# Memory projection between the steps of the causal latent attention; token sums of squares made on PE

## The reference, cut to what matters

```python
mla_out = _rms_norm(_latent_attention(q_m, k_m, v_m), mla_out_g[l])      # 8 heads, causal
x = x + jnp.concatenate([diff_out, mla_out], axis=-1) @ w_out[l]
x = x + _memory_cross_attention(_rms_norm(x, norm_cross_g[l]), _rms_norm(mem, norm_mem_g[l]),
                                w_mem_q[l], w_mem_kv[l], w_mem_o[l])
x = x + _hierarchical_moe(_rms_norm(x, norm_ffn_g[l]), ...)
...
x = _rms_norm(x, norm_final_g)          # end of the first block
h = rms_norm(x, ln_mix[0])              # start of the second
proj = h @ w_in                         # 3072 + 12 + 256 columns; the 12 are the gates b and a
```

## Time and profile before

| | |
|---|---|
| median of 3 runs | 2022.97 us (2021.37 to 2024.80) |
| the profiled execution's own time | 2024.49 us |
| its span in the profile | 2022.2 us |
| PE busy | 1881.0 us (93%) |
| DVE, ACT, POOL busy | 1056.4, 759.7, 123.1 us |
| instructions | 27340 |
| moved by DMA | 248.58 MB, 410 GB/s at most in a fortieth of the span |

### The profile page before, as it was taken

One profiled execution on the slowest core, in us unless ns is written; L12 is line 12 of the kernel. 1 busy time (PEld: TensorE's weight loads), 2 busy tenths in 40 slices (PEclk: granted clock), 3 DMA queues, 4 the chain that ended last, 5 costly groups with the idle time before them and its releaser, 6 DMA issues.

```text
span 2022.2 us, 27340 instructions
## 1 busy us (share of the span) xinstructions
PE 1881.0 (93%) x10882; PEld 1447.1 (72%) x10882; DVE 1056.4 (52%) x2003; ACT 759.7 (38%) x1606; POOL 123.1 (6%) x108
## 2 busy tenths in 40 slices
PE   6999888998997859999879999999999999999997
PEld 5665567786554437778777888888876688888886
DVE  6757656353211157775655444644567654444444
ACT  4455744441111146523443322322345542222222
POOL 0000000001212135010210000000000000000000
PEclk9999988999999969999999999999999999999998
DMA  5101213349999942122002233232321132323321
GB/s 192 43 10 31 89 45 110 141 149 400 410 410 408 402 173 74 61 66 74 2 1 85 90 103 94 86 112 89 99 73 43 32 105 94 104 92 95 95 94 42
DMA packets 72621, 248.58 MB, mean 123 GB/s; under 512 B 9218, under 2 KB 11522, under 8 KB 71600
## 3 DMA queue, kind: packets, MB, share of 16 engines
q1 hardware_dynamic: 67088, 235.65, 33.2%
q0 software_dynamic: 5408, 11.19, 1.6%
HBM read 242.62 MB, written 12.59 MB: 126 GB/s over the span
## 4 chain that ended last, share of the span: by engine, by line
PE 74%; DVE 7%; DMA 4%; ACT 3%; issue 1%; POOL 0%; DVEq 0%; POOLq 0%; SPq 0%; ACTq 0%
PE ps_pair L299 18%; PE ps_pair L300 18%; PE ps_pair L301 18%; PE ps_pair L2050 5%; DMA w_places<-w_experts 2%; PE ps_turn L2661 2%; PE ps_pair L892 1%; PE ps_out L2061 1%; PE ps_shared L2061 1%; DMA split_acts_as_f<-w_experts 1%; PE ps_out L923 1%; PE ps_pair L2653 1%; DVE g L2461 1%; PE ps_turn L904 1%; DMA g<-rows_h,g_as_int 1%
## 5 line engine op out<-in xcount | busy, mean ns | idle before, releaser
L299 PE MATMUL ps_pair<-split_acts,w_high 128*128 128x512 f32 (+1 forms) x1816 | 722.5, 398 | 25.0 <-DVE split_acts L626 13.2
L301 PE MATMUL ps_pair<-split_acts,w_low 128*128 128x512 f32 (+1 forms) x1816 | 706.0, 389 | 0.0
L300 PE MATMUL ps_pair<-split_acts,w_high 128*128 128x512 f32 (+1 forms) x1800 | 699.8, 389 | 0.0
L299 PEld LDWEIGHTS ps_pair<-split_acts,w_high 128*128 128x128 f32 x1816 | 344.5, 190 | 106.9 <-issue 27.2
L242 DVE TENSOR_TENSOR w_low<-w_raw,w_high 128x1024 fp32r<-128x1024 f32 (+4 forms) x249 | 281.6, 1131 | 258.2 <-ACT w_high L236 256.3
L301 PEld LDWEIGHTS ps_pair<-split_acts,w_low 128*128 128x128 f32 x1816 | 344.0, 189 | 72.2
L300 PEld LDWEIGHTS ps_pair<-split_acts,w_high 128*128 128x128 f32 x1800 | 342.3, 190 | 67.7 <-issue 1.9
L236 ACT ACTIVATE w_high<-w_raw 128x1024 fp32r<-128x1024 f32 (+4 forms) x249 | 242.8, 975 | 145.5 <-PE ps_pair L301 143.2
L372 DVE TENSOR_TENSOR x<-x,ps_pair 128x512 f32<-128x512 f32 x80 | 55.0, 687 | 140.6 <-PE ps_pair L301 140.6
L2288 DVE TENSOR_TENSOR g<-g,ps_pair 64x256 f32<-64x256 f32 x31 | 13.2, 425 | 177.1 <-ACT g L2232 177.1
L3254 ACT ACTIVATE split_acts<-h 128x512 fp32r<-128x512 f32 x44 | 27.9, 633 | 200.1 <-DVE h L3267 200.1
(11 more groups left out here) (562 smaller groups left out, 2392.9 us busy)
## 6 DMA issues: line engine op xcount, KB each, us to landing
w_raw<-w_gu SPq DMA_DIRECT2D x88, 512.0 KB, 3.5
split_acts_as_f<-w_experts SPq DMA_DIRECT2D x42, 1024.0 KB, 19.4
w_places<-w_experts SPq DMA_DIRECT2D x35, 1024.0 KB, 20.3
w_raw<-w_down SPq DMA_DIRECT2D x32, 448.0 KB, 3.2
w_raw<-w_gdnin SPq DMA_DIRECT2D x26, 512.0 KB, 3.6
w_raw<-w_out SPq DMA_DIRECT2D x24, 512.0 KB, 3.6
x<-w_experts SPq DMA_DIRECT2D x12, 1024.0 KB, 20.2
w_raw<-w_down SPq DMA_DIRECT2D x16, 512.0 KB, 3.5
```

The source lines that it names most:

```text
L299: pe.matmul(out, wh[:, k, :], self.high(k), start=(n == 0), stop=False)
L300: pe.matmul(out, wh[:, k, :], self.low(k), start=False, stop=False)
L301: last = pe.matmul(out, wl[:, k, :], self.high(k), start=False, stop=(n == self.kt - 1))
```

## The change

Two parts, in one kernel.

*A.* `memkv` moves ahead of `out` in the order of stages. The latent attention is cut in 19 steps of `gap`, with the one bank pair that `ps_lin` leaves. Steps 0 to 3 run with the memory norm (its squares at step 1, root at 2, outputs at 3), steps 4 to 18 in the middle of and beside the eight tiles of `memkv`. The norm's sum and spread use a `ps_lin` bank. The parts of `at_group` are placed anew. `n_cross` becomes `Deferred`: its products by gain and squares stand beside the tiles of `out`, and `memq` is scaled by the root when DVE takes it. Buffers move accordingly, and with them what some loads wait for.

*B.* The row of the final gain, POOL's products by it and ACT's squares of token rows go. ACT squares the transposed tiles from PSUM instead, and PE makes from them both sums of squares, as two more columns beside the 12 gate columns, for each tile of 128 tokens: tile 0 after the second transposes, tiles 1 and 2 after the fourth, tile 3 after `gdnin` tile 0. Their turn stands in `gdnin` tile 1, roots and gates after it, attention scores after tile 2, decay sums in tile 3, decays after tile 3 and in tile 4. The reciprocal root is also written to four columns of `ROWS` instead of one.

```diff
-          ("ukv", MLA_HEADS, 1, P, S), ("out", KT, KT, P, S),
-          ("memkv", 8, KT, P, NMEM), ("memq", 4, KT, P, S), ("memo", KT, 4, P, S),
+          ("ukv", MLA_HEADS, 1, P, S), ("memkv", 8, KT, P, NMEM),
+          ("out", KT, KT, P, S), ("memq", 4, KT, P, S), ("memo", KT, 4, P, S),
           ("gdnin", 26, KT, P, S), ("out0", KT, KT, P, S)]
...
-                before = m - (len(self.banks) if n >= len(self.banks) else 2)
+                before = m - (len(self.banks) if n >= len(self.banks) or self.after else 2)
...
-        for k in range(len(mla.groups)):
-            mla.number(k)
-            mla.beside[k] = []
+        mla.banks = pairs[1:]
...
+        out_hi = lambda k: GR[:, 8 + k, :] if k < 4 else AR[:, 4 + k, :]
...
-            [head_norm.finish(1), high(0), head_norm.spread(2)],
-            [head_norm.finish(2), low(0), high(1), head_norm.spread(3)],
-            [head_norm.finish(3), low(1), high(2), square(2)],
-            [low(2), high(3), added(2)],
-            [low(3)]]
-        for k, stages in enumerate(at_group):
-            mla.beside[k + 1] += stages
-        fl += [mla, n_mo.part(3), n_mo.root(), n_mo.spread()]
-        n_cross = Norm("cross", KT, S, x_tile, lambda k: vec("norm_cross", k), h_tile, hi, lo,
-                       lambda e: wait_stage_evac(e, "out"),
-                       wait_dst=lambda e: (wait_products(e, "out")), early=True)
-        memv = lambda k0: G[:, k0:k0 + 4, :].rearrange("p k (a s) -> p (k a) s", a=2)
-        raw1 = memv(20)
-        mh = AR[:, 24:28, :].rearrange("p k (a s) -> p (k a) s", a=2)
-        ml = AR[:, 28:32, :].rearrange("p k (a s) -> p (k a) s", a=2)
+            [head_norm.finish(1), head_norm.spread(2)],
+            [head_norm.finish(2), head_norm.spread(3)],
+            [head_norm.finish(3), square(2)],
+            [high(0), high(1), added(2)],
+            [low(0), low(1), high(2), high(3)],
+            [low(2), low(3)]]
+        memv = lambda f: f.rearrange("p k (a s) -> p (k a) s", a=2)
+        raw1, mh, ml = memv(G[:, 20:24, :]), memv(AR[:, 0:4, :]), memv(GR[:, 20:24, :])
         n_mem = Norm("mem", KT, NMEM, lambda k: raw1[:, k, :], lambda k: vec("norm_mem", k),
                      lambda k: raw1[:, k, :], lambda k: mh[:, k, :], lambda k: ml[:, k, :],
-                     lambda e: (load_waits(e, "mem"), last_head(mla)(e)))
-        n_mem.sq = n_mem.total = H[:, 0:4, :].rearrange("p k s -> p (k s)")
-        n_mem.wait_src = lambda e: (load_waits(e, "mem"), need(e, *n_mo.ready(3)), need(e, *s_diff.ready(3)))
-        mk = memv(8)
+                     lambda e: load_waits(e, "mem"))
+        n_mem.sq = n_mem.total = AF[:, 0:4, :].rearrange("p k s -> p (k s)")
+        n_mem.bank = ps_lin[(BASE["memkv"] + 1) % BANKS]
+        mem_squares, mem_root, mem_out = n_mem.steps()
+        mem_k, mem_v_rows = memv(G[:, 6:8, :]), memv(AF[:, 20:22, :])
+        mem_at = lambda j: mem_k[:, j, :] if j < 4 else mem_v_rows[:, j - 4, :]
+        MEM_FROM = 4
+        mla_gaps = [[mla.gap(n)] + (at_group[n - 3] if 0 <= n - 3 < len(at_group) else [])
+                    for n in range(len(mla.groups) + 3)]
+        mla_gaps[1].append(mem_squares)
+        mla_gaps[2].append(On(tensor=lambda pe: wait_stage_evac(pe, "ukv")))
+        mla_gaps[2].append(mem_root)
+        mla_gaps[3].append(mem_out)
+        fl += [stage for here in mla_gaps[:MEM_FROM] for stage in here]
+        mem_beside, mem_middle = defaultdict(list), defaultdict(list)
+        for n, here in enumerate(mla_gaps[MEM_FROM:]):
+            (mem_beside if n % 2 else mem_middle)[n // 2] += here
+        fl.append(Linear("memkv", lambda k: mh[:, k, :], lambda k: ml[:, k, :], n_mem.ready, taker(mem_at),
+                         beside=mem_beside, middle=mem_middle))
+
+        def handed_over(pe):
+            held.append(mla.last)
...
+        hi_q = lambda k: AR[:, 24 + k, :]
+        lo_q = lambda k: AR[:, (16, 17, 22, 23, 6, 7)[k], :] if k < 6 else GR[:, (1, 3)[k - 6], :]
+        n_cross = Deferred("cross", lambda k: vec("norm_cross", k), hi_q, lo_q, lambda e, k: wait_evac(e, BASE["out"] + k))
...
-                         *add_and_square(n_cross), beside=in_steps(n_mem, 0, 2, 4)))
-        fl.append(Linear("memkv", lambda k: mh[:, k, :], lambda k: ml[:, k, :], n_mem.ready,
-                         taker(lambda j: mk[:, j, :]), beside=in_steps(n_cross, 0, 0, 1)))
-        fl.append(Linear("memq", hi, lo, n_cross.ready, taker(lambda j: g(4 + j))))
+                         n_cross.take_act, n_cross.take_dve))
+        fl.append(n_cross.rest())
+        q_at = (4, 5, 14, 15)
         mem_v = Transposes("mem_v", [
-            ([(mk[:, 4 + c, i * P:(i + 1) * P], c * P) for c in range(4)], (g(12 + i), lambda b: b[:, :]), None)
+            ([(mem_v_rows[:, c, i * P:(i + 1) * P], c * P) for c in range(4)], (g(12 + i), lambda b: b[:, :]), None)
             for i in range(2)], wait_first=lambda e: wait_stage_evac(e, "memkv"))
+        fl.append(Linear("memq", hi_q, lo_q, n_cross.ready, None, scaled(lambda j: g(q_at[j])), opening=n_cross))
...
-                first = {0: lambda: wait_products(sp, "memkv"), 2: lambda: need(sp, *n_cross.ready(KT - 1)),
-                         3: lambda: wait_products(sp, "memq"), 5: lambda: need(sp, *cross.last),
+                first = {0: lambda: wait_products(sp, "memq"), 1: lambda: need(sp, "turn_act", mem_v.t0 + 1),
+                         2: lambda: wait_stage_evac(sp, "memq"), 5: lambda: need(sp, *cross.last),
...
-                    if b == 12:
-                        final_row_tensor(pe)
...
-            need(pool, "row_act", 1)
-            for i in range(QT):
-                need(pool, "comb_dve", ("sum", i))
-                done(pool.tensor_tensor(YG(i, 0), ROWS[:, i, 0:D], FINAL_ROW, ALU.mult), "comb_pool", ("gained", i))
...
+        def columns_tensor(pe, i):
+            need(pe, "comb_act", ("square", i, 1))
+            need(pe, "comb_dve", "columns")
+            n = slice(i * P, (i + 1) * P)
+            for w, x in ((W_GROUPS, X[:, :, n]), (S_GROUPS, SQUARES(i))):
+                for k in range(KT):
+                    group = slice(GRP * (k % 4), GRP * (k % 4) + GRP)
+                    last = pe.matmul(ps_m[group, n], w[:, k, :], x[:, k, :], start=(w is W_GROUPS and k < 4),
+                                     stop=(w is S_GROUPS and k >= 4), skip_group_check=True)
+            if i == QT - 1:
+                done(last, "ba_pe", "rows")
...
             for i in range(QT):
                     ba_rows_tensor(pe)
                 need(pe, "comb_dve", ("sum", i))
                 if i >= 2:
-                    need(pe, "comb_act", ("x", i - 2, 1))
+                    need(pe, "comb_act", ("square", i - 2, 1))
                 for k in range(KT):
                     last = pe.transpose(banks_of(i)[k // 4][:, (k % 4) * P:(k % 4 + 1) * P],
                                         ROWS[:, i, k * P:(k + 1) * P], ident)
                     if k % 4 == 3:
                         done(last, "comb_pe", (i, k // 4))
+                for n in {1: (0,), 3: (1, 2)}.get(i, ()):
+                    columns_tensor(pe, n)
 
         def combine_scalar(act):
             ss1, ss2 = ROOTS[:, 32:36], ROOTS[:, 36:40]
             act.activation(ROOTS[:, 63:64], col(C_EPS), ACT.Sqrt)
+            by_feature = lambda i, q: banks_of(i)[q][:, :].rearrange("p (c t) -> p c t", t=P)
+
...
+            def squares(i):
+                for q in range(2):
+                    done(act.activation(SQUARES(i)[:, 4 * q:4 * q + 4, :], by_feature(i, q), ACT.Square), "comb_act",
+                         ("square", i, q))
             for i in range(QT):
                 for q in range(2):
                     need(act, "comb_pe", (i, q))
-                    done(act.copy(X[:, 4 * q:4 * q + 4, i * P:(i + 1) * P],
-                                  banks_of(i)[q][:, :].rearrange("p (c t) -> p c t", t=P)), "comb_act", ("x", i, q))
+                    done(act.copy(X[:, 4 * q:4 * q + 4, i * P:(i + 1) * P], by_feature(i, q)), "comb_act", ("x", i, q))
                 if i < QT - 1:
-                    squares(act, i)
+                    squares(i)
             n_mix0.scalar(act)
-            squares(act, QT - 1)
-            need(act, "comb_act", ("ss2", QT - 1))
-            done(act.activation(ss1, ss1, ACT.Sqrt, bias=col(C_EPS), scale=1.0 / D), "comb_act", "std1")
+            squares(QT - 1)
+            need(act, "ba_pe", "rows")
+            done(act.copy(BA_ROWS, ps_m[:, :]), "ba_act", "rows")
+            act.wait_ge(ba_done, QT)
+            done(act.activation(ss1, BA[:, :, SUM1], ACT.Sqrt, bias=col(C_EPS), scale=1.0 / D), "comb_act", "std1")
             need(act, "comb_dve", "scaled")
             done(act.activation(ss2, ss2, ACT.Sqrt, bias=col(C_EPS), scale=1.0 / D), "comb_act", "std2")
-
-        def squares(act, i):
-            done(act.activation(YG(i, 1), ROWS[:, i, 0:D], ACT.Square, accum_out=ROOTS[:, 32 + i:33 + i]), "comb_act",
```

(20 more changed lines are left out.)

73 lines of the change are left out of this document (26 added, 47 removed).

## The result

The changed kernel takes 2031.7 us (median of 11 runs, 2028.5 to 2035.4), the kernel before 2023.3 in the same session: a ratio of 1.0035, 95% interval 1.0026 to 1.0043, so 7.1 us slower (5.3 to 8.7). The profiled execution's own time is 2032.1, its span 2030.1.

What follows compares the result with a forecast made beforehand. PE, busy 93% of the span, was taken as the bound, so only its idle and half-clock stretches could yield time. A +0.7 and B -1.4 sum to -0.7: 2022.97 becomes 2022.3 us, range 2013 to 2030.

Steps and rivals of the forecast that it cites:

- A, the steady part: Latent attention's last 14 steps beside `memkv`: 56.7 us of PE work plus 3.0 of idle, between 0 and 8.
- A, the opening: Attention's first steps with the memory norm: first projection tile done after 31.5 us, 18.2 of them lost; bounds 12 and 24.
- Tail: From the last value products to `out`: 5.0 us, bounds 3.5 and 6, where it was 5.5.
- `out` to the transposes: `out` runs 46.7 less 0.8 us, then transition and queries take 24.0 to the memory transposes.
- SP's late pieces and POOL: Load queues before the experts: later expert pieces and `mem2_t` cost nothing; 7.7 us if the pieces were missed.
- The slower one: Latent attention: the single bank pair makes the steps latency-bound; 2029.3 us, chance 0.27.
- The faster rival: Opening loses only 12 us, and PE is at full clock before `gdnin` in the combine; about 2013.6 us, chance 0.32.
- Sums at 1.22: Combine: without POOL each DVE sum takes 1.22 us, the fourth load's sums done at 738.8, not 744.9: -6.1.
- The column products: PE before `gdnin`: column products of tiles 0 to 2, and transposes waiting for squares, give back 1 to 6 us.
- Tile 0 ends: First `gdnin` tile: ends 4.5 us earlier than 757.54, bounds 0.5 and 7.2.
- After tile 0: `gdnin` behind tile 0: gates' columns, turn and roots moved, 10.9 us where it was 11.3, -0.4.
- The wait before the decays: PE reaches `decay(0)` 3 to 5 us before DVE's gates are ready: +3.5, bounds 0 and 5.

Runs made afterwards that it cites:

- one_pair: `behind_out` with a single pair of score banks for the latent attention where it has two; ratio 1.0067, 25 us slower than `behind_out`.
- no_switch: The changed kernel with the square roots of memory norm and head norm taken as copies, so without six table loads; ratio 1.0004.
- behind_out: The changed kernel with `memkv` back behind `out` and the attention in its own two-pair order, cross norm still deferred, combine as changed; ratio 0.9943, median 2013.5 us.
- b_alone: Only the combine's edits (part B) on the kernel before; ratio 0.9987, 2.6 us faster.

## Why the prediction was wrong, step by step

Forecast 2022.3 with a range of 2013 to 2030; it became 2031.7. The sum said A +0.7 and B -1.4; the traces say A +8.2 and B -2.7.

**A, the steady part: the step that failed.** It is the term of 3.0 us for PE's waits in the fourteen steps behind the opening. From the first projection tile done (250.9) to the last projection product (318.1) it is 67.3 us; the prediction had 56.7 of work and 3.0 of waits, 59.7, so 7.6 too few, and with the upper bound of 8 for the waits 64.7, still too few. PE is busy 59.1 of it, 2.4 more than the work at full clock; I estimate 1.7 of them from 283 to 289, where PE is busy throughout at a granted clock of 0.72. The rest are waits, 8.1 us. PE's waits in this part, kernel after (in all, times, longest):

```profile
PE ps_pair L894 <- ACT g L959: 4.6, 4, 2.0
PE ps_shared L1554 <- DVE h L1505: 2.6, 2, 1.5
PE ps_out L925 <- ACT split_acts_as_f L975: 0.9, 1, 0.9
```

Three things were mis-sized. First, the waits for exponentials and for the copy before the values, without the table load's 1.5 us, come to 4.1 where I had 3.0. The nearest row, 3.84 idle of 120, is the sum of the stretch from 80 to 200 of the kernel before (not of the three stretches shown above it in the earlier trace rows). It came from stepping beside products of 512 columns, where the half tile between steps is 2.7 us (half of 24 products at 0.23); here it is 1.4, as the prediction itself says two clauses earlier. Over the whole attention the waits for exponentials are 8.0 us with this cover and 13.9 with none (`one_pair`); a larger cover was not run. Second, the head norm's root and its two table loads: 242.89 stands in the earlier trace rows, hidden by scores two groups ahead, and I used the row for the price of a load only, without asking who hides that very load once one pair is gone. `no_switch` puts it at 2.6, wait and half clock together. Third, DVE's head norm outputs, 2.6 us of waits at 291.79 and 297.56, placed newly among the steps, had no term. These three make 6.3 of the 7.6; the rest is busy time that no run divides.

**A, the opening.** Predicted 31.5 us to the first projection tile, measured 32.1, with PE waits at the memory norm's sum, the exponentials and its low parts as the queues were followed. There are four table loads in it, not three; without them it is 28.0. That the sum is so near is partly luck: the projection begins 24.1 us after the first scores, where 22 were said, and its first tile then takes 8.0 instead of 9.5.

**A, tail, transition, queries.** Tail 5.0 predicted, 5.4 measured (318.1 to 323.5). `out` to the transposes 69.9 predicted, 68.8 measured; at the deferred norm's sums and spreads there is no idle time, as the earlier trace rows let expect. SP's late pieces and POOL: no wait of the experts answers to them. These terms hold.

**The rivals.** The slower one (0.27, 2029.3) is nearest in size, and its mechanism is shown in part: `one_pair` shows that a single pair makes the steps wait, and the root's loads come on the chain where the second pair had hidden them. But of the 7.5 us that A takes beyond the forecast only 1.1 are plain waits of the steps and 2.6 the root's; the 2.6 of the head norm's outputs are waits for DVE, of which I had said nothing. I had it decide "from the point where minimum, exponential and the copies ahead exceed PE's 4 us a step" and weighed it down by the same row of 120 us. `one_pair` shows its weight without cover, 25 to 29 us. The faster rival was right in one half: in the combine PE is at full clock before `gdnin`, and tile 0 takes 5.6 us, not 8.2.

**B.** Sums at 1.22: right (what POOL had made beside them were the products by the gain, not squares, as the prediction once calls them). The transposes of the last token tile come 9.0 us after the first ones, not 13.7: 4.7 earlier, predicted 6.1, since DVE waits 1.46 for the last load. The column products cost nothing: from these transposes to `gdnin` it is 3.6 us, before 4.4. Tile 0 ends 8.0 earlier (18.2 us after the first transposes, before 26.2), outside my bound of 7.2, though the gain at the sums was smaller: the full clock in tile 0, 2.6 us, was no term of my sum. After tile 0 it is 10.3 us to tile 2, where it was 11.3 (predicted -0.4, came -1.0). The wait before the decays is 3.94, predicted 3.5, in the place named and for DVE; but behind it PE runs at half clock again (0.77 us for the product at 790.25), so from tile 2 to the key norm 6.4 us are given back. In sum -2.7 where -1.4 was said: two larger terms, of opposite sign.

**The range.** A and B each fell inside their bounds, and 2022.97 with 8.2 and -2.7 is 2028.5, inside the range too. The 3.2 us from there to 2031.7 belong to neither place in the traces. 0.3 of them is the kernel before, whose median was 2023.3 in the later session; the rest stays open, and the range, "not all met at once", had no room left for it.

**What stays open.** A and B make 5.5 us, the comparison says 7.1 (5.3 to 8.7), so its interval holds 5.5. From the memory transposes to the gate rows behind the last expert product it is 340.2 and 338.0 us in the two traces of the kernel before, 339.5 and 342.1 in those of the changed one, 342.0 in `behind_out` and 336.9 in `b_alone`. That spread can hold the rest, and the 4 us that `behind_out` lacks, but one or two traces of each don't tell whether the later loads have a share. Of the 20.2 us by which the changed kernel's attention and projection exceed those of `behind_out` (104.7 against 84.5), an experiment gives 6.6 to the table loads; how the rest divides between the single pair, the memory norm in the opening and the head norm's outputs is read from waits only.

## What to carry to other kernels

Before work is laid between the steps of a latency chain, ask which resource the steps give up for it: here a second pair of banks, worth 25 to 29 us where nothing covers the steps, for a cover of 1.4 us a step. An idle share is to be read at a place with the same cover and the same neighbours in the queues, and each operation that was hidden (a table load, a norm's output) is to be asked again who hides it now. Of two queues that feed each other, each half of a pair belongs one step later than the other: the same work took 24.5 us less that way. And when a move brings with it a second edit, try that edit alone: the deferred norm with `memkv` left behind `out`, together with B, is 11.5 us faster than the kernel before.

## What the runs showed of the hardware that I had not expected

Waits of 0.2 to 3.9 us before the scores of 12 of 16 groups brought the granted clock of a whole stretch from 0.87 to 0.71, and PE's busy time rose by 16.8 us for the same instructions, more than the 12.4 of idle time. Unchanged code ahead of the change ended between 214.2 and 219.7 us. Of these 5.6 us, 4.0 are there by the first scores of the first attention (33.3 to 37.3), where the traces differ in when the first product starts (9.5 to 11.9) and in a stretch at half clock between 17 and 30 us that lasts 3 to 10 us. A single pair of traces can show 4 us that belong to no edit.
